# Gathered token rows turned by VectorE in 32x32 blocks, in the expert loop of a trunk layer

## The reference

```
h = rmsnorm(x, g_pre_ffn) * (1 + sc2) + sh2            # 640 tokens x 1024
scores = sigmoid(h @ w_router)                          # 64 experts
idx = top 8 of 64 (within 4 of 8 groups); wts = scores[idx] / sum * 2.5
for each block of tokens of one expert e:
    xb = h[toks]                                        # gather
    hb = silu(xb @ w_e_gate[e]) * (xb @ w_e_up[e])      # 1024 -> 256, twice
    acc[toks] += (hb @ w_e_down[e]) * gates             # 256 -> 1024
out = acc + shared expert
```

## Time and profile before

| What | Value |
|---|---|
| Median of 3 runs | 1332.42 us (1331.71 to 1336.72) |
| Profiled execution | span 1333.0 us; the page gives no other time of its own |
| VectorE busy | 529.4 us (40%) |
| ScalarE busy | 317.9 us (24%) |
| GpSimd busy | 315.0 us (24%) |
| Bytes moved by DMA | 350.43 MB, mean 263 GB/s |
| Expert loop, first down to last | 543.6 to about 1254 us of the span |

### The profile page before, as it was taken

One profiled execution on the slowest core, in us unless ns is written; L12 is line 12 of the kernel. 1 busy time (PEld: TensorE's weight loads), 2 busy tenths in 40 slices (PEclk: granted clock), 3 DMA queues, 4 the chain that ended last, 5 costly groups with the idle time before them and its releaser, 6 DMA issues. The chain is left out here.

```text
span 1333.0 us, 26899 instructions
## 1 busy us (share of the span) xinstructions
PE 1263.8 (95%) x8920; PEld 717.0 (54%) x8920; DVE 529.4 (40%) x1714; ACT 317.9 (24%) x696; POOL 315.0 (24%) x385
## 2 busy tenths in 40 slices
PE   4999999889989999999999999999999999999777
PEld 3535544667845544555555555555555555555344
DVE  1265068695704464333233232332232332323157
ACT  4121111274122222222222222222222222222111
POOL 4021230230010000333333333333333333333100
PEclk9899899997999999999999999999999999999889
DMA  9944943774155232924994999999999999673196
GB/s 351 276 157 159 248 154 126 248 173 153 33 214 220 95 142 77 369 83 148 372 409 167 382 396 364 413 364 414 377 416 374 412 405 386 269 285 132 54 430 266
DMA packets 109579, 350.43 MB, mean 263 GB/s; under 512 B 33125, under 2 KB 39028, under 8 KB 90080
## 3 DMA queue, kind: packets, MB, share of 16 engines
q1 hardware_dynamic: 87344, 302.54, 59.7%
q0 software_dynamic: 20608, 45.09, 9.1%
q10 hardware_dynamic: 1584, 2.23, 0.5%
HBM read 484.98 MB, written 47.52 MB: 399 GB/s over the span
## 5 line engine op out<-in xcount | busy, mean ns | idle before, releaser
L1988 PE MATMUL banks<-rings,hT 128*64 128x256 f32 x3712 | 420.3, 379 | 3.2 <-DMA rings<-w_e_up 1.3
L1988 PEld LDWEIGHTS banks<-rings,hT 128*64 128x64 f32 x3712 | 265.5, 137 | 186.8 <-issue 69.0
L2011 PE MATMUL banks<-downs,hT 128*64 128x512 f32 x928 | 224.3, 605 | 1.0 <-issue 0.4
L1851 POOL DMA_INDIRECT h<-h2D,toks x117 | 118.2, 1010 | 414.9 <-DVE kept L1915 402.3
L1878 ACT ACTIVATE hT<-banks 128x512 f32<-128x512 f32 x116 | 69.3, 597 | 375.5 <-PE banks L1975 375.4
L1864 POOL DMA_INDIRECT yD<-hT,dest x116 | 118.0, 1017 | 134.0 <-ACT hT L1892 131.0
L1948 DVE COPY hT<-banks 128x128 f32<-128x128 f32 x116 | 33.9, 292 | 285.3 <-PE banks L1999 285.3
L1892 ACT ACTIVATE hT<-banks,gain 128x512 f32<-128x512 f32 x116 | 79.7, 687 | 182.3 <-PE banks L2011 182.3
L2011 PEld LDWEIGHTS banks<-downs,hT 128*64 128x64 f32 x928 | 56.9, 138 | 69.0 <-issue 68.9
L1905 DVE COPY info<-wparts 128x20 bf16 x118 | 21.6, 183 | 154.8 <-issue 153.7
L1631 PE MATMUL banks<-rings,mixedT 128*128 128x512 f32 x160 | 71.1, 604 | 3.7 <-PEq L2184 3.7
(11 more groups left out here) (453 smaller groups left out, 1445.0 us busy)
## 6 DMA issues: line engine op xcount, KB each, us to landing
rings<-w_e_gate SPq DMA_DIRECT2D x116, 1024.0 KB
rings<-w_e_up SPq DMA_DIRECT2D x116, 1024.0 KB
downs<-w_e_down SPq DMA_DIRECT2D x116, 1024.0 KB
rings<-w_ada SPq DMA_DIRECT2D x12, 2048.0 KB, 10.3
rings<-yD SPq DMA_DIRECT2D x7, 2048.0 KB, 17.8
rings<-w_in SPq DMA_DIRECT2D x4, 2048.0 KB, 11.5
rings<-matD SPq DMA_DIRECT2D x3, 2048.0 KB, 12.5
matD<-rings SPq DMA_DIRECT2D x2, 2048.0 KB, 6.9
```

The costliest lines, as they stand in the source:

```text
L1851: pool.indirect_dma_start(out=xg[u], out_offset=None, in_=k.h2D, bounds_check=2 * TOK - 1, oob_is_err=False, in_offset=bass.IndirectOffset ...
L1988: last = pe.matmul(bank[par][h * SB:(h + 1) * SB, 0:F].rearrange("p (x f) -> p x f", x=2), lhsT=lhsT, rhs=w[:, kk, :, h * FH:(h + 1) * FH] ...
L2011: last = pe.matmul(bank[4 + par][h * SB:(h + 1) * SB, :], lhsT=hidT[par][:, kk, :], rhs=down[:, kk * D + h * 512:kk * D + (h + 1) * 512], ...
```

## The change

Named part by part; none of the arithmetic of gate/up, down, silu or the router changes.

- `h2D` holds a token as four rows of 256 values. `route` writes `h2` in plain order, and its TensorE transposes read every eighth column instead (L1640).
- A block fetches quarter rows. `toks` has two columns, and `gather` issues two indirect DMAs, one for each column. Partitions are four groups of 32: which quarter a partition fetches follows from its group (`k.quarter`) and the column.
- `tokens` makes the columns' own entries; the entries that another group of partitions needs are copied across by `swaps`, four instructions on 32 partitions each. ScalarE does these in the loop (with the offset as its bias), VectorE in the head of the loop.
- TensorE's `turn` and ScalarE's `turned` go. VectorE's new `turned` is one block transpose of 128x512 from `xg` to `xT`. It stands behind the product and ahead of the wait for the hidden transpose, and `onehot` of block i+6 now stands there too, right behind it.
- TensorE does the hidden transpose of block i within gate/up of block i+1, ahead of its sixth step of eight.

More of the change, by code:

```diff
@@ L63 @@
 SB = 64
+QB = 32
 MAXB = TOK // SB
@@ L1440, in _ @@
         pl(pool.memset(k.half[SB:P, :], float(OFF + 1)))
-        iota(k.ids[:, :, 0], [[2 * P, NT]], -OFF, 0)
-        iota(k.ids[:, :, 1], [[0, NT]], 0, 2)
+        for a_ in range(4):
+            pl(pool.memset(k.quarter[a_ * QB:(a_ + 1) * QB, :], float(OFF + a_)))
+        iota(k.ids[:, :, 0], [[4 * P, NT]], -OFF, 0)
+        iota(k.ids[:, :, 1], [[0, NT]], 0, 4)
         iota(k.ids[:, :, 3], [[2 * TOPK * P, NT]], -OFF, 0)
@@ L1639, in turn @@
             for kk in range(KD):
-                last = pe.transpose(bank[4 + kk // 4][:, (kk % 4) * P:(kk % 4 + 1) * P], h2[t % 2][:, kk * P:(kk + 1) * P], ident[:, :])
+                last = pe.transpose(bank[4 + kk // 4][:, (kk % 4) * P:(kk % 4 + 1) * P], h2[t % 2][:, kk:D:KD], ident[:, :])
             last.then_inc(h2_t, 1)
@@ L1763, in experts @@
     found = [sb(f"found{i}", [P, 3]) for i in range(2)]
-    toks, dest = ([sb(f"{n}{i}", [P, 1], I32) for i in range(U)] for n in ("toks", "dest"))
+    toks, dest = ([sb(f"{n}{i}", [P, w], I32) for i in range(U)] for n, w in (("toks", 2), ("dest", 1)))
     kept = [sb(f"kept{i}", [P, 2]) for i in range(U)]
@@ L1875, in _ @@
     def _(act):
-        def turned(it, u):
-            act.wait_ge(xg_t, it * U + u + 1)
-            act.activation(xT[u % 2], bank[2][:, :], ACT.Copy).then_inc(xT_ready, 1)
         act.wait_ge(k.shared_out, 2 * NT)
-        turned(0, 0)
-        turned(0, 1)
         act.wait_ge(k.table_ready, 1)
@@ L1913, in tokens @@
             dve.wait_ge(found_ready, i + 1)
-            dve.tensor_scalar(toks[u][:, :], f[:, 0:1], k.half[:, :], None, ALU.add)
+            dve.tensor_scalar(toks[u][:, :], f[:, 0:1].to_broadcast([P, 2]), k.quarter[:, :], None, ALU.add).then_inc(own_ready, 1)
             dve.tensor_copy(kept[u][:, :], f[:, 1:3]).then_inc(toks_ready, 1)
+            if spread:
+                dve.wait_ge(own_ready, i + 1)
+                for held, other, g, offset in swaps:
+                    last = dve.tensor_scalar(toks[u][other, g:g + 1], f[held, 0:1], offset, None, ALU.add)
+                last.then_inc(spread_ready, 1)
+        def turned(it, u):
+            i, par = it * U + u, u % 2
+            dve.wait_ge(gathered[u], it * 32 + 32)
+            if not (first(it) and u < 2):
+                dve.wait_ge(gu_ready, i - 1)
+            dve.transpose(xT[par].rearrange("p (k g j) -> p g k j", k=KD, g=2),
+                          xg[u].rearrange("p (g i k) -> p g k i", g=2, k=KD)).then_inc(xT_ready, 1)
         def late(it, u):
@@ L1967, in ids, with gate_up @@
             last.then_inc(ids_ready, 1)
-        def turn(it, u):
-            i = it * U + u
-            pe.wait_ge(gathered[u], it * 16 + 16)
-            if not (first(it) and u == 0):
-                pe.wait_ge(xT_ready, i)
-            for j in range(4):
-                last = pe.transpose(bank[2][:, j * P:(j + 1) * P], xg[u][:, j * P:(j + 1) * P], ident[:, :])
-            last.then_inc(xg_t, 1)
-        def gate_up(it, u):
+        def gate_up(it, u, between=None):
             i, par = it * U + u, u % 2
```

26 lines of the change are left out of this document (14 added, 12 removed).

## The result

The changed kernel takes 1313.4 us (median of 4 runs, 1309.13 to 1318.12), the kernel before in the same comparison 1332.8 us (4 runs, 1331.71 to 1336.72). The ratio is 0.987, with an interval of 0.983 to 0.990. The forecast was 1308, range 1290 to 1333. The profiled execution took 1313.49 us, with a span of 1311.7.

What follows compares the result with a forecast made beforehand. TensorE was taken to bound all blocks, with weight transfers right behind in 48 of 116. Savings of 19.4 (free periods) and 6.5 (rhythms) less 1.2 (descriptors), 24.7 off 1333.0, gave 1308 us; range 1290 to 1333.

Steps and rivals of the forecast that it cites:

- TensorE loses the transposes: Expert loop: four transposes of gathered rows leave TensorE, 0.53 us a block, so it alone would need 5.64 instead of 6.17.
- VectorE becomes the bound: Expert block: down waits for VectorE's hidden copy, starting at 4.14 instead of 3.90 us; period 5.88, saving 0.29 a block.
- rival 1: Expert loop: TensorE stays the bound at period 5.64 if lookups begin earlier or run shorter by 0.25 us; 1292 us, chance 0.13.
- lookup stretch: VectorE's two table lookups ahead of the one-hot, running beside the block transpose: 1.66 us after it is sent.
- 67 free periods: Expert-loop blocks where transfers do not stand right behind TensorE: 67 x 0.29 = 19.4 us saved.
- The rhythms: Four 12-block stretches, 8 blocks loading experts and 4 skipping, DMA 98 or 99% busy: 1.6 us saved each, 6.5 together.
- Descriptors: Gathers in saturated stretches: twice as many descriptors of half the size add 5%, 0.03 us a block, 1.2 us in 48 blocks.
- rival 3: Gathers: quarter rows cost the DMA engines double, 6.2 us more per 12 blocks; about 1331 us, chance 0.11.
- ScalarE and GpSimd at nothing: Expert loop: ScalarE's four index copies (at most 1.2 us) and GpSimd's third indirect DMA (1.01 us) cost no time.
- Rival 4: Saturated stretches: gathered rows land late, VectorE and then TensorE wait, the gain goes there; about 1328 us, chance 0.05.
- Routing and head at nothing: Before the loop: in-order row writes counted nothing, at most 2 us; loop head taken as 0, bound -2 to +2.
- Rival 2: VectorE's block transpose is dear, costing from 1.57 us and deciding at 1.86; 1392 us, chance 0.17 with a serial-lookup variant.

Runs made afterwards that it cites:

- half-row kernel: Changed kernel with one gather of half rows per block instead of two of quarter rows, from an index column of its own: 1305.4 us, ratio 0.980.
- second profile: Profile of the changed kernel run again unaltered, beside the other experiments: 1312.6 us, ratio 0.988 to the kernel before.
- split kernel: Kernel before with each block's gather split into two indirect DMAs of quarter rows, still turned on TensorE: 1335.0 us, ratio 1.002.

## Why the prediction was right, and where its terms were not

The time came within 5 us of the forecast, and a good part of that is luck. All terms of the sum, 24.7 us, were savings in the loop, and the loop's profiles show 13.9 and 18.5 us (712.7 before, 698.8 and 694.2 after). The rest of the 21.3 us between the first two profiles lies ahead of the loop and behind it, 4.7 of it in stages that the change doesn't touch. Within the loop three terms were off and partly cancelled.

- **TensorE loses the transposes: right in direction, wrong in size.** It alone was to need 5.64. It needs 5.77, because gate/up in two parts takes 3.60 instead of 3.55 and the hidden transpose 0.26 instead of 0.17, inside the matmul stream. I had the split at nothing. It is still worth its price, since with the hidden transpose at the end the period is 6.12.
- **VectorE becomes the bound: wrong.** I had the one-hot's copy at 3.05 and down at 4.14 (period 5.88, a wait of 0.24 for VectorE); it came at 2.82, down at 4.02, and down waits for VectorE 0.4 us in all. The mechanism is rival 1's, held at 5.77 by the split. The transpose was right, 1.10 against an estimate of 1.0 with ends of 0.55 and 1.8. What was too long was the lookup stretch: 1.45 us after the transpose was sent (692.94 to 694.39), not 1.66. That lookups run beside the instruction ahead is shown twice, by the changed kernel's 0.35 of idle time and by the doubled transpose that leaves none.
- **67 free periods: the sum right (19.5 against 19.4), not its parts.** They gained 0.395 each, 26.5 in all, and about 7 came back outside the four rhythms, where I had said that TensorE alone is the bound: two waits for weights (1.7 and 3.2 us) and a block at half clock behind the second.'s mean share of 0.82 over the loop should have warned me: bursts of loads stand there too.
- **The rhythms: wrong.** I had 6.5 us off and 1.2 on; the profile has 5.6 on. Per rhythm, on average: of the 1.9 us from landing to need 1.1 was given up, where I had counted on 1.6. The other 0.7 can't be had: a gate/up that waited for its weights started 0.7 to 0.9 us behind their last packet, in the old kernel too, so 1.6 was too much from the start. From issue to landed took 1.4 longer (68.7 to 70.1). Of that the half-row kernel puts 0.6 down to the smaller descriptors, and about 0.7 are bytes: at the rate of the kernel before it moved 28.0 MB in that stretch and not 27.8. An estimate of where they come from: with the shorter period 12 blocks and not 11 gather and scatter in it, with 0.39 MB each (45.1 MB by 116). And from the wanted gate/up to the next rhythm's first issue 5.15 instead of 3.97 passed: 0.45 by the longer gate/up with the hidden transpose in it, and in the third and fourth rhythm 1.3 to 1.6 more, where that gate/up ran at half clock. Such a wait is paid twice, as the wait and as the slow block after it, which holds back the next load. But only four of the ten waits in this profile brought half clock (those of 3.22, 3.38, 3.17 and 3.02 us), and another of 3.17 us did not; in the second profile one of 2.15 us did. What decides it the runs don't show. The kernel before had one wait of about 1.3 us there and no half clock up to the last gate/up.
- **Descriptors: under-sized.** I had 5% of the gathers, 0.3 us a rhythm, from equal shares per MB. By the rates the split kernel shows 1.3 us a rhythm, about 0.11 us a block and a fifth of the 0.52 that I gave the gathers, and the changed kernel 0.6. The Trainium skill (DMA: Bandwidth & Descriptors, section Bandwidth) has small transfers dominated by descriptors; the runs agree in direction, at a tenth to a fifth of the doubling that rival 3 took from it. The share of a queue is the time of its packets. It is 9.4% in the changed kernel both with quarter and with half rows, so it isn't the measure of what the gathers cost the loads beside them. Why, the records don't show, and that stays open.
- **ScalarE and GpSimd at nothing: right.** Four copies take 0.84 us (I had at most 1.2), and it makes no difference who does them. GpSimd's third issue hides in 5.77. Rows were never late in the loop: VectorE waited for a gather only ahead of the first block (1.9 us), and no gate/up started within 2.8 us of the end of its block's transpose. Rival 4 did not occur.
- **Routing and head at nothing: right.** VectorE's rows fell from 2003 to 1284 ns, and from the first matmul of route to the first gate/up the time is 0.9 us shorter.
- **Rival 2: further off than I had it.** With the doubled transpose (2.17 us) the period is 6.01; microsecond for microsecond from there it would be 6.18 at about 2.35 us, an estimate, where I had 1.86. The Trainium skill's 311 ns for a 128x128 bf16 tile on VectorE (VectorE: DVE Perf Modes, The three transpose paths) gives an estimate of 1.24 for four; 1.10 was measured, for float32 and with the strided read in it.

What stays open: why the split lowered the rate by 1.9% in the old kernel and by under 1% in the changed one; which waits bring half clock; and the 376.9 to 384.9 us of the untouched front stages. That spread is larger than the forecast's error, so a single profile's total can't confirm a term; the loop's own length can.

## What to carry to other kernels

Before taking work off the bounding engine, find the second bound in each stretch and ask how far below the first it lies; where transfers are at 98% and land 2 us early, 2 us less the time from landing to start is all there is, whatever the engine gains. Running past that point can cost something on top, here 5.6 us in four rhythms; the half-row kernel, whose blocks are as short, took 298.5 us there against 298.4 before. Work that looks like overhead may be the cover of a round trip to another engine: here the removal was worth 0.07 us a block and the reordering that had to go with it 0.33. Measure the engines' side of a change with the loads switched off; the difference tells what the transfers take back.

## What the runs showed of the hardware

- Behind a wait of 3.17 us TensorE's granted clock fell from 2.4 to 1.2 GHz for 3.4 us, and the gate/up that ran in it took 5.7 us instead of 4.1 (first start to last end). Behind another wait of 3.17 us in the same profile it did not fall.
- VectorE's 32x32 block transpose of 128x512 float32 takes 1.10 us at a read stride of 8 and 0.71 in order.
- Register loads of VectorE's sequencer run beside the engine's instruction ahead, about 1 us of them here.
- With the same rows gathered in twice as many descriptors, saturated load bursts moved 400 GB/s instead of 403.5 (changed kernel) and 396.5 instead of 404 (old one), with the gathers' queue at 9.4% of the DMA engines' time in both changed kernels, and at 9.3% against 9.1% in the old one.
- A gate/up that waited for its weights started about 0.2 us behind their semaphore and 0.7 to 0.9 us behind their last packet.
- A 32x1 ScalarE copy costs 0.20 us, four in a row 0.84 us.
